# Every second low half of the weights, outside the convolution layers, computed on Pool in place of DVE

## What is computed

```
# first block: x = x + mixer(rms_norm(x)) for a0, b, c, a1
a: val, gate, z = split(h @ w_in, 3); u = val * sigmoid(gate)
   u = silu(layer_norm(causal_conv31(u) + bias)); out = (u * silu(z)) @ w_out
b: q, k, v, z, f = split(h @ w_in); 16 heads of forgetting attention; (o * silu(z)) @ w_out
c: u, b, c, z = split(h @ w_in, 4); (b * causal_conv3(c * u) * silu(z)) @ w_out
# second block, twice: mod = silu(c_2) @ w_ada + b_ada gives shifts, scales and gains
m: h @ w_in -> 8 heads with top-k selection and relative bias, 8 latent heads with rope;
   merged = sigmoid(ga) * (ya @ w_branch_a) + sigmoid(gb) * (yb @ w_branch_b); merged @ w_out
   x = layer_norm(ALPHA * x + g1 * y)
f: u = causal_conv3(h @ w_up) + b; (silu(g) * val) @ w_down; x = layer_norm(ALPHA * x + g2 * y)
```

## Time and profile before

| | |
|---|---|
| median of 3 runs | 2077.12 us (2076.99 to 2078.76) |
| the profiled execution | 2082.0 us |
| its span | 2080.2 us |
| busy in the span | PE 91%, weight loads 82%, DVE 78%, ACT 52%, POOL 14% |
| mean granted TensorE clock | 0.962 of full speed |
| layers in the span, about | a0 to 249, b to 608, c to 860, a1 to 1098, m0 to 1351, f0 to 1599, m1 to 1856, f1 to 2067 us |

### The profile page before, as it was taken

One profiled execution on the slowest core, in us unless ns is written; L12 is line 12 of the kernel. 1 busy time (PEld: TensorE's weight loads), 2 busy tenths in 40 slices (PEclk: granted clock), 3 DMA queues, 4 the chain that ended last, 5 costly groups with the idle time before them and its releaser, 6 DMA issues.

```text
span 2080.2 us, 32564 instructions
## 1 busy us (share of the span) xinstructions
PE 1895.7 (91%) x12370; PEld 1702.1 (82%) x12370; DVE 1620.2 (78%) x3041; ACT 1079.7 (52%) x1928; POOL 301.1 (14%) x380
## 2 busy tenths in 40 slices
PE   7897999989999999989979988988887987889997
PEld 6897888868889899889968876877886986779996
DVE  6988788978889998599976866778888576686666
ACT  6887644423354444478855444444445444454554
POOL 3876000000000000087800000020001000010000
PEclk9998999989999999999989999999999999999998
DMA  6344455634446776344535632537775352344652
GB/s 219 124 162 132 162 183 186 229 111 142 132 139 219 236 236 204 112 139 145 171 111 162 206 110 82 183 121 268 273 266 181 122 151 78 103 161 153 206 189 71
DMA packets 93756, 342.29 MB, mean 165 GB/s; under 512 B 10400, under 2 KB 10528, under 8 KB 92960
## 3 DMA queue, kind: packets, MB, share of 16 engines
q1 hardware_dynamic: 93600, 340.20, 49.9%
HBM read 339.11 MB, written 1.05 MB: 164 GB/s over the span
## 4 chain that ended last, share of the span: by engine, by line
PE 56%; DVE 30%; ACT 11%; issue 2%; DMA 0%; POOL 0%; SPq 0%; DVEq 0%; ACTq 0%
PE ps L98 55%; DVE wl L114 9%; ACT tmp L104 6%; DVE ps L124 5%; DVE tmp L124 3%; ACT wh L107 3%; DVE B L124 2%; DVE XS L114 2%; DVE tmp L114 1%; DVE B L114 1%; DVE tmp L119 1%; DVE raw L124 1%; ACT B L104 1%; DVE sm L136 1%; PE ps L101 1%
## 5 line engine op out<-in xcount | busy, mean ns | idle before, releaser
L98 PE MATMUL ps<-XS,wh 128*128 128x256 f32 (+1 forms) x5072 | 955.2, 290 | 39.9 <-DVE wl L114 27.4
L98 PEld LDWEIGHTS ps<-XS,wh 128*128 128x128 f32 (+1 forms) x5072 | 807.9, 195 | 65.4 <-issue 40.6
L114 DVE TENSOR_TENSOR wl<-raw,wh 128x1024 fp32r<-128x1024 f32 (+1 forms) x493 | 591.8, 1228 | 180.5 <-ACT wh L107 180.5
L98 PE MATMUL ps<-XS,wl 128*128 128x256 f32 (+1 forms) x2536 | 726.6, 287 | 0.0
L107 ACT CAST wh<-raw 128x1024 fp32r<-128x1024 f32 (+1 forms) x493 | 496.0, 1038 | 98.6 <-PE ps L98 92.8
L98 PEld LDWEIGHTS ps<-XS,wl 128*128 128x128 f32 (+1 forms) x2536 | 495.4, 195 | 0.0
L114 POOL TENSOR_TENSOR B<-B,tmp 128x236 f32<-128x236 f32 (+10 forms) x352 | 268.3, 800 | 775.1 <-ACT tmp L104 775.1
L98 PE MATMUL ps<-wh,os 128*128 128x512 f32 x864 | 291.0, 405 | 27.8 <-DVE os L114 18.9
L124 DVE SCALAR_TENSOR_TENSOR ps<-B,C,ps 128x254 f32<-128x254 f32 (+17 forms) x576 | 224.5, 469 | 8.3 <-ACT ps L104 8.3
L98 PEld LDWEIGHTS ps<-wh,os 128*128 128x128 f32 x864 | 167.9, 194 | 67.0 <-DVE os L114 20.8
L98 PE MATMUL ps<-wl,os 128*128 128x512 f32 x432 | 173.4, 401 | 0.0
(11 more groups left out here) (155 smaller groups left out, 1950.2 us busy)
## 6 DMA issues: line engine op xcount, KB each, us to landing
raw<-in_w SPq DMA_DIRECT2D x623, 512.0 KB, 4.4
raw<-in_w SPq DMA_DIRECT2D x12, 384.0 KB, 3.9
B<-in_ln SPq DMA_DIRECT2D x4, 1024.0 KB, 6.8
C<-in_cst SPq DMA_DIRECT2D x1, 1309.5 KB, 8.2
X<-in_x SPq DMA_DIRECT2D x2, 512.0 KB, 4.6
out_x<-X SPq DMA_DIRECT2D x4, 256.0 KB, 2.5
cb<-in_cb SPq DMA_DIRECT2D x1, 512.0 KB, 13.2
raw<-in_w SPq DMA_DIRECT2D x2, 256.0 KB, 3.3
```

Source lines behind the costliest of these rows:

```text
L98: return NOTHING if self.e is None else self.e.matmul(*a, **k)
L114: return NOTHING if self.e is None else self.e.tensor_tensor(o, a, b, op)
```

## The change

Per layer, the split pieces are counted from 0; those with an odd number of 5 or more are put into the set `on_pool`, except in a0 and a1. That is 194 pieces: 38 in b, 38 in c, 28 in m0, 31 in f0, 28 in m1, 31 in f1 (188 of 1024 columns, four of 768, two of 512). `feed_dve` skips them; the new `feed_pool` subtracts them on Pool, each behind a wait for its cast. They count on a semaphore of their own, `poollow`, and `low(i)` gives `load` and `weights` the right one. Pool's list gets the pieces of b and c between the convolution layers' taps, and those of the other layers ahead of the `pool_norm` of the same layer.

```
+POOL_FROM = 5
...
+            if kind == "split" and stage[0] != "a":
+                n[stage] = n.get(stage, -1) + 1
+                if n[stage] >= POOL_FROM and n[stage] % 2:
+                    self.on_pool.add(i)
...
+    def low(self, i):
+
+        return self.s["poollow" if i in self.on_pool else "low"][i]
...
-                sp.wait_ge(*self.s["low"][j])
+                sp.wait_ge(*self.low(j))
...
-            if self.kind[i] == "split":
+            if self.kind[i] == "split" and i not in self.on_pool:
...
+    def feed_pool(self, pool, stage):
+        s = self.s
+        for i in sorted(self.on_pool):
+            if self.pieces[i][0].split(".")[0] == stage:
+                pool.wait_ge(*s["cast"][i])
+                hi = self.m["wh"][i % NHL][:, 0:self.wd[i]].bitcast(F32)
+                pool.tt(self.m["wl"][i % NHL][:, 0:self.wd[i]], self.raw(i), hi, ALU.subtract).then_inc(
+                    s["poollow"].up(i), 1)
...
-        pe.wait_ge(*self.s["low"][i])
+        pe.wait_ge(*self.low(i))
...
         self.pool_a(pool, 0)
+        self.feed_pool(pool, "b")
+        self.feed_pool(pool, "c")
         self.pool_a(pool, 1)
         for L in ("m0", "f0", "m1"):
+            self.feed_pool(pool, L)
             self.pool_norm(pool, L)
+        self.feed_pool(pool, "f1")
```

## The result

The changed kernel takes 2134.47 us (median of 4 runs, 2126.09 to 2137.18) against 2077.46 (2076.99 to 2078.76): ratio 1.027, 95% interval 1.024 to 1.030. Slower, as forecast, but by 57 us where 22 were forecast, and above the range (2078 to 2126). The profiled execution took 2133.56 us, its span 2131.0.

A forecast was written before the change was run, and what follows sets the result against it. DVE's throughput bounds c until 795 us, PE bounds f1, a latency chain m's attention loops; PE is 91% busy overall. c +25, b +5, m -14, f0 +5, f1 +1 make +22 on 2077.1: 2099 us, range 2078 to 2126.

The forecast's parts named there:

- second estimate: Pool's time for a 1024-wide low half taken from the Trainium skill: 2.25 us, making c's gain term below 1.5 us smaller.
- the five periods: Stage c, 640 to 795 us, at DVE's pace: each 31 us period grows by 5.0 us, together +25 us.
- (C): Rival: gains in m whole, a fifth of c's blocking hidden; c +18, m -20, sum +1, 2078 us; chance 0.09.
- the first period and those after 795 us have room: Stage c outside its DVE-bound periods: blocking fits into DVE's idle time, 33.8 of 35 us, so no growth.
- it waits for one DVE operation (up to 1.2 us): Stage c: Pool's start is delayed by at most one DVE operation, then 2.34 us of work, so results are not late.
- the term of 0.5 us for each later head: Attention loops of m0 and m1: four moved heads from 8 on gain 0.5 us each, 2.0 per layer.
- a DVE operation with two SBUF inputs waits: All stages: such operations wait for a Pool operation under way, 2.18 us of blocking each; in c, PSUM-input ones do not.
- Elsewhere in the layer +0.4: m0 and m1 outside the attention loop's gain and the layer's end: a loss of 0.4 us per layer.
- The step that was named: f0: Pool finishes piece u.1.0 later than DVE did, +0.5 us a pair, ten pairs, +5 us.
- (A): Rival: one Pool operation costs DVE only 0.5 us, below the 1.135 saved; sum -26, 2051 us; chance 0.12.
- (B): Rival: Pool slower, 2.67 us, and b without room; c +34, b +14, sum +47, 2124 us; chance 0.17.
- (D): Rival: Pool's pieces wait behind pool_norm or the taps, costing PE several us at once; about 2110 us; chance 0.04.

The follow-up runs named there:

- experiment 5: Kernel before with accumulating bias steps cut to 64 of 384 columns: ratio 0.9906; the same with stage c's 38 pieces on Pool: 0.9976.
- experiment 6: Pool also waits for DVE's nearest earlier kept low half: whole change 1.0203, only c's pieces moved 1.0104, those with thinned bias steps 0.9943, against the kernel before.
- c alone: Only the 38 pieces of stage c go to Pool, against the kernel before: ratio 1.0163, c +30.7 us.
- m alone: Only the 56 pieces of m0 and m1 go to Pool, against the kernel before: ratio 0.9997, m0 -0.1, m1 +0.7 us.
- experiment 4: Only the pieces of f0 and f1 except u.0.1 go to Pool, against the kernel before: ratio 1.0018, f0 +4.8 us.
- experiment 2: Kernel before, DVE keeping all low halves, plus 38 extra Pool operations in c on buffers of their own: ratio 1.0227, c +45.3 us.
- experiment 3: Only c's pieces on Pool, each as two 512-column operations instead of one of 1024, against the kernel before: ratio 1.0116, c +25.7 us.
- b alone: Only the 38 pieces of stage b go to Pool, against the kernel before: ratio 1.0095, b +17.0 us.
- f alone: Only the 62 pieces of f0 and f1 go to Pool, against the kernel before: ratio 1.0035, f0 +5.1 us.

## Why the prediction was wrong, point by point

**Price of one operation: right.** 2.34 us was taken; the 39 low halves on Pool that began while DVE stood took 2.34 to 2.42, in the median 2.40. The blocking of 2.18 us was 2.14 in the median in c's full periods. The prediction's second estimate, 2.25 us, is below all of them; with it the five periods would lose some 2.1 us less, not the 1.5 that the prediction says. The low ends of c do not come out either (2.15 us with a fifth hidden gives +12, not +15, and 2.34 with a fifth hidden +15, not (C)'s +18). Nothing else hangs on these.

**Stage c, +25 forecast, +32.8 measured.** The five periods were right: from pair 2 to pair 12 they lost 24.5 us. In four of them (pair 2 to pair 10) DVE's busy time rose from 30.5 to 35.6 us a period, by the 5.0 that was forecast, and its idle time by 0.5. The step that failed is "the first period and those after 795 us have room". They lost 4.1 and 4.2 us (2.6 of these in a wait of PE for DVE's low half of `z12.1`, 1.6 behind it with the clock at its lower level for 3.4 us). DVE's idle time in a window is no room for blocking where the blocking comes right behind a cast, and that is where DVE's next low half is due: the timeline of experiment 5 shows it, and with the wait of experiment 6 the first period loses 1.0 us in place of 3.1 (c alone) and the stretch after 795 1.7 in place of 2.7. For `z12.1` itself it is not shown. Nor is the rate one of throughput for every order: with the wait the five periods lose 18.0 us in place of 24.8 (c alone).

**Stage b, +5 forecast, +14.9 measured.** The failed step is one half-sentence in the part on c: "it waits for one DVE operation (up to 1.2 us)". Of 188 low halves of 1024 columns 185 last 3.4 us at most, which is that; two last 4.2 and 5.2, and one waits behind 14 operations, and 9.8 us come in there (7.8 at `q4.0`, 2.0 behind it). Without that place b is at +5, the forecast (2.9 in `v`, the rest in the late pieces). That is arithmetic and no run: with `q4.0` left on DVE another piece was passed, and b was at +9.6.

**m0 and m1, -14 forecast, about 0 measured.** The gain of the loop was sized right: m0 goes from +2.1 to -6.6 us between `g0` and `g11`, 8.7, m1 8.2 to `g9`; forecast 8.5. Of that forecast 2.0 us were for the four later heads, and these did not give them.

Two steps failed. The first is the term of 0.5 us for each later head, and behind it "a DVE operation with two SBUF inputs waits": the `tensor_scalar` operations with one SBUF input wait too, `sc<-B` 2.48 us in place of 0.35, the scaling of the scores 2.63 in place of 0.55. From `g9` to `bs0` PE's waits are 1.5 (m0) and 0.7 us (m1) longer than before, where some 1.5 less were forecast. The second is a term that the prediction put at nothing: PE's own pace. In that same stretch PE's own instructions take 2.8 and 6.8 us longer, with the clock at its lower level for 7 and 17 us where it was at the upper one throughout.

Over the whole layers PE's waits fall by 5.0 and 4.2 us, and its instructions take 4.8 and 4.9 longer. In m1 the lower level lasts 27.3 us here and with m alone, and 13.7 to 18.6 in the kernels with nothing changed in m, so it may be an effect of the change; in m0 the kernels with nothing changed have 7 to 22 us, and it can be chance. "Elsewhere in the layer +0.4" was +1.2 at `qk3` of m0 alone, where Pool's low half is ready 1.2 us later than DVE's was and PE takes it at once, and 1.5 more at `qk4`, which is the clock; the end of m0 cost 1.8, not 1.1.

**f0, +5 forecast, +4.5 measured; f1, +1, nothing measured.** The size is right, and f1 too. The step that was named is real (experiment 4: 0.58 us a pair when it stands alone), but in the changed kernel a delay that was not foreseen stands in front of it (the down piece 1.07 us late, 0.47 given back at `u.1.0`). That both come to 0.6 us a pair is luck.

**Rivals.** (A) is out: experiment 2. (B), the slower Pool, would have given about the measured total for a wrong reason. (D) did not occur. None of the rivals had a lower clock in it. The 6 us by which the timed runs miss more than the profile (57 against 51) lie within the scatter of the changed kernel, whose runs differ by 11 us where those before, beside them, differ by 2; what makes them scatter was not tried, but the fastest (2126.09 us) has the highest mean clock, 0.959 against 0.954 to 0.956.

## What to carry to other kernels

Moving an elementwise operation from VectorE to GpSimd paid only where VectorE waited at that very place of the program anyway: here 14 of the 194 moved pieces, taken while it waited for exponentials (-17 us); those of f1 changed nothing, the others cost. A busy share does not tell this; look in the timeline at what VectorE does in the 2.4 us behind the event that releases GpSimd, and whether that is needed sooner than what GpSimd makes. If work is shared nevertheless, let GpSimd wait for the earlier piece, and try shorter operations. And a forecast for a kernel at 91% of TensorE needs a term for its clock: of 51 us here 16 are TensorE's own instructions, which the change did not touch.

## What the runs showed of the hardware

- A Pool operation on SBUF keeps DVE from its next operation on SBUF until Pool's is done, wherever the two's data lie (experiment 2), for one instruction at a time (experiment 3: 1.1 us with 512 columns, 2.2 with 1024). DVE's `tensor_scalar` operations with one SBUF input (128x384 and 128x256 columns of float32) are kept out as those with two; convolution steps with an input in PSUM are not. The Trainium skill (SBUF — State Buffer, section SBUF: two separate sides) says whoever starts first holds the port pair for the whole instruction; the trace agrees for 2.15 of Pool's 2.40 us.
- The other way round there is no fair turn. Pool nearly always comes in behind the operation of DVE under way (185 of 188), but where DVE's operations follow one another without a gap it was passed by 14 of them, 9.8 us, at the same place in each of three kernels, and by 7 at a neighbouring place in a fourth. What decides when Pool gets in is open.
- Two Pool operations of 512 columns stretch DVE no more (2 x 1.05 us) than one of 1024 (2.15), though they take longer (2 x 1.27 against 2.40).
- The same code takes 1.5 us more where the granted clock falls for 3.4 us. Windows of m0 (`qk0` to `va0`) in two kernels whose code is the same up to there, with the pieces of f but `u.0.1` moved, and with the twelve of the loop moved (the clock is the number before the last two):

```profile
1145.00:1185.00 40.00, 35.07 (x253) 32.85 (x252) 32.16 (x66) 19.25 (x27) 0.00 (x0) 1.00 0.64 214
```

```profile
1145.00:1185.00 40.00, 35.06 (x242) 32.96 (x241) 30.86 (x61) 18.35 (x26) 0.00 (x0) 0.96 0.62 209
```

A mean of 0.96 is one stretch of 3.4 us at the lower level of 1.2 GHz in place of 2.4; PE's three waits in it are the same (2.44, 1.58, 0.92 us). PE reaches `qk4` 1.5 us later in the second, and so it does in the runs with c alone and with the extra operations, where nothing is moved in m0; in those with b alone and f alone it does not. A difference of 1.5 us in one stage of one profile says nothing by itself.
